# Eight gate units of the merge beside the last two RWKV pairs, and the pooling of the even layer beside its matrix units

## The reference

```python
# first block
proj = h @ w_in                         # attention, RWKV and gate columns
y_att  = attention_mixer(att_in) @ w_att_out
y_rwkv = rwkv7_mixer(rwkv_in, ...) @ w_rwkv_out
g_att, g_rwkv = split(sigmoid(gate_in + b_gate))
x = x + gt1 * ((g_att * y_att + g_rwkv * y_rwkv) @ w_o)
# ... conv ffn, norm; second block, layer 0 (the even layer)
proj = xn @ w_in_even                   # a_b, a_c, a_v (512 each), z_b (512)
y_a = a_b * causal_dwconv3(a_c * a_v, conv_w)
# y_b: for each of 4 groups of 128 channels, window w in (2, 4, 8, 16)
pooled = (cs - shifted) / minimum(pos, w) - z      # mean of the last w tokens, minus z
y_b = einsum(pooled, w_pool) * pool_scale
h = h + concat(y_a, y_b) @ w_out_even
```

## Time and profile before

| | us |
|---|---|
| median of 3 runs (lowest, highest) | 2472.72 (2471.85, 2472.84) |
| the profiled execution | 2470.49 |
| its span | 2469.3 |
| PE busy in the span | 2337.9 (95%) |
| DVE, POOL, ACT busy | 1433.1, 882.9, 686.1 |

### The profile page before, as it was taken

One profiled execution on the slowest core, in us unless ns is written; L12 is line 12 of the kernel. 1 busy time (PEld: TensorE's weight loads), 2 busy tenths in 40 slices (PEclk: granted clock), 3 DMA queues, 4 the chain that ended last, 5 costly groups with the idle time before them and its releaser, 6 DMA issues.

```text
span 2469.3 us, 33874 instructions
## 1 busy us (share of the span) xinstructions
PE 2337.9 (95%) x14384; PEld 1847.0 (75%) x14384; DVE 1433.1 (58%) x1805; ACT 686.1 (28%) x854; POOL 882.9 (36%) x415
## 2 busy tenths in 40 slices
PE   6999998999998799899999988999999999999998
PEld 4776775666665688678888866888888887888887
DVE  4221324577667411766675568888863457888733
ACT  3222113434442423222222221322222332322212
POOL 4322221111110344344444433444444444444443
PEclk8999999999999899989999989999999999999999
DMA  6433332212110333223333323233333322333331
GB/s 235 128 103 111 111 103 68 51 41 51 43 45 14 107 98 94 86 77 94 98 112 94 90 62 88 86 102 95 95 110 95 93 86 85 98 98 94 113 94 58
DMA packets 412038, 222.56 MB, mean 90 GB/s; under 512 B 33823, under 2 KB 409458, under 8 KB 410610
## 3 DMA queue, kind: packets, MB, share of 16 engines
q1 hardware_dynamic: 387234, 208.23, 29.2%
q10 hardware_dynamic: 24656, 12.18, 1.8%
HBM read 214.61 MB, written 5.77 MB: 89 GB/s over the span
## 4 chain that ended last, share of the span: by engine, by line
PE 59%; DVE 6%; issue 1%; ACT 1%; POOL 0%; DVEq 0%; ACTq 0%
PE bank L309 59%; DVE ev_s L2406 0%; DVE h_low L2014 0%; DVE mg_r_low L1992 0%; DVE g_c L2216 0%; PE bank L312 0%; DVE ev_low L2418 0%; DVE x_res L2363 0%; DVE sq L653 0%; DVE sq L649 0%; DVE ev_z L2373 0%; DVE ev_c L2375 0%; DVE ev_c L2382 0%; DVE ev_s L2409 0%; DVE sq L2113 0%
## 5 line engine op out<-in xcount | busy, mean ns | idle before, releaser
L305 POOL TENSOR_TENSOR w_low<-w_raw,w_high 128x1024 fp32r<-128x1024 f32 (+1 forms) x331 | 849.5, 2568 | 1494.7 <-ACT w_high L298 1494.6
L309 PE MATMUL bank<-h_high,w_high 128*128 128x512 f32 x2008 | 809.0, 403 | 28.4 <-DVE h_low L660 9.6
L309 PE MATMUL bank<-h_low,w_high 128*128 128x512 f32 x2008 | 789.3, 393 | 0.0
L298 ACT CAST w_high<-w_raw 128x1024 fp32r<-128x1024 f32 (+1 forms) x331 | 358.5, 1084 | 913.2 <-PE bank L309 899.6
L309 PE MATMUL bank<-h_high,w_low 128*128 128x512 f32 x2008 | 510.5, 394 | 0.0
L309 PEld LDWEIGHTS bank<-h_high,w_high 128*128 128x128 f32 x2008 | 379.9, 189 | 133.7 <-issue 24.8
L309 PEld LDWEIGHTS bank<-h_high,w_low 128*128 128x128 f32 x2008 | 377.0, 189 | 84.2 <-issue 4.6
L309 PEld LDWEIGHTS bank<-h_low,w_high 128*128 128x128 f32 x2008 | 381.3, 190 | 78.1 <-issue 3.4
L309 PE MATMUL bank<-g_high,w_high 128*128 128x512 f32 x352 | 138.1, 392 | 2.3 <-ACT g_c L2195 2.3
L309 PE MATMUL bank<-g_low,w_high 128*128 128x512 f32 x352 | 137.8, 391 | 0.0
L2092 DVE TENSOR_TENSOR x_res<-bank,x_res 128x512 f32<-128x512 f32 x32 | 22.1, 692 | 164.8 <-PE bank L309 164.8
(11 more groups left out here) (375 smaller groups left out, 2886.2 us busy)
## 6 DMA issues: line engine op xcount, KB each, us to landing
w_raw<-in_w_in SPq DMA_DIRECT2D x58, 512.0 KB, 4.7
w_raw<-in_w_up SPq DMA_DIRECT2D x44, 512.0 KB, 3.8
w_raw<-in_w_ffn_gate SPq DMA_DIRECT2D x44, 512.0 KB, 3.8
w_raw<-in_w_ffn_up SPq DMA_DIRECT2D x44, 512.0 KB, 3.8
w_raw<-in_w_ffn_down SPq DMA_DIRECT2D x32, 704.0 KB, 4.5
w_raw<-in_w_ada SPq DMA_DIRECT2D x32, 512.0 KB, 3.6
w_raw<-in_w_down SPq DMA_DIRECT2D x16, 704.0 KB, 4.5
w_raw<-in_w_in ACTq DMA_DIRECT2D x21, 512.0 KB, 4.1
```

Of the source, the lines that this page charges most:

```text
L298: self.A.copy(self.w_high[:, u % SPLIT_SLOTS, 0:k * P], self.raw_of(key)[:, 0:k * P]).then_inc(*self.S.rounded(*key))
L305: self.G.tensor_tensor(self.w_low[:, slot, 0:k * P], self.raw_of(key)[:, 0:k * P], self.w_high[:, slot, 0:k * P].bitcast(F32), ALU.subtrac ...
L309: return self.T.matmul(out, lhsT, rhs, start=start, stop=stop, skip_group_check=True)
```

## The change

**Merge.** The eight gates (n, 0) and (n, 1) for n = 0 to 3, called u = 0 to 7 here, come first in the order of units. u0 and u1 are woven in beside the chain and the mean of pair 6, u2 beside the solve of pair 7, u3 beside its chain, u4 beside its mean and variance (`EARLY`); u5 to u7 run right behind. Their sigmoids go to the tiles of `x` instead of `masks_room`. ACT's casts and sigmoids for them are placed by hand in `recurrence_act` and `merge_act`; POOL subtracts seven of them in the recurrence. The meetings of the engines before the merge go; each split is waited for by tile (`ready`), where it is used. The transfer of `x` waits for the fourth merged tile, `both` 3.

**Even layer.** The pooling of group g comes right behind its multiplication by the root; the table of counts becomes 16 reciprocals made at the start (`few`). The product with `w_pool` comes before the unit (n, 0); ACT makes the high parts of both results, DVE the low ones; the residual is scaled two tiles at a time; `even_out` takes tiles 4 to 7 first and no longer waits for ACT's last instruction. In `f_down`, `h_low` is written before the last scaling and squares.

Left out of the diff below: the declarations of tiles, the setup of `few` (POOL: one iota of 16 and four small copies at the start; DVE: one reciprocal of 128x64 with the RWKV vectors), and lines that only follow from those shown.

```diff
-        for n in range(DT):
...
-            unit(("merge", n, 3), wr, n * P)
+        for n, j in self.merge_order():
+            if j < 2:
...
         for n in range(4):
             for j in (1, 2, 0):
+                if j == 0:
+                    ring.append((("w_pool", n), [(0, 0, None, io["w_pool_2"][0, n])], None))
                 unit(("even", n, j), even, n * P + j * 4 * P)
-            ring.append((("w_pool", n), [(0, 0, None, io["w_pool_2"][0, n])], None))
...
+        order = self.TILE_ORDER.get(key[0], range(tiles))
...
     def recurrence_pe(self):
...
-        later = lambda i, j, b: self.projected_pe(i, j, b) if has(i) and i else iter(())
+        def later(i, j, b):
+            if has(i):
+                return self.projected_pe(i, j, b) if i else iter(())
+            return self.early_gate_pe(self.EARLY[i, j]) if (i, j) in self.EARLY else iter(())
...
+    GATES_EARLY = 8
+    EARLY = {(DT, IN_K): 0, (DT, IN_R): 1, (DT, IN_V): 2, (DT + 1, IN_K): 3, (DT + 1, IN_R): 4}
...
+    def merge_order(self):
+        early = [divmod(u, 2) for u in range(self.GATES_EARLY)]
+        return early + [(n, j) for n in range(DT) for j in range(4) if (n, j) not in early]
...
+    def early_gate(self, u):
+
+        return ("merge",) + divmod(u, 2), 7 - u % 2, self.x[:, u, :]
+
+    def early_gate_pe(self, u):
+        key, b, _ = self.early_gate(u)
+        self.empty(b)
+        yield from self.product_steps(key, self.bank[b][:], *self.h_parts())
+        self.emptied[b] = (self.S.gate_open, key[1:])
+        yield
...
+    def early_gate_act(self, u):
+        key, b, tile = self.early_gate(u)
+        _, n, j = key
+        if u == 0:
+            self.A.wait_ge(*self.S.dve_arrive.at("mixed", DT - 1))
+        self.A.wait_ge(*self.S.product.at(*key))
+        self.A.activation(tile, self.bank[b][:], ACT.Sigmoid, bias=self.col("b_gate", n + j * DT)).then_inc(*self.S.gate_open(n, j))
...
     def recurrence_act(self):
         has = self.has
         for i in range(-2, DT + 1):
             if has(i + 1):
                 self.rwkv_loads(("g2", i + 1), ("w2a2", i + 2), ("rwkv", i + 2, IN_K))
+            if i == DT - 2:
+                for u in range(3):
+                    self.load_gate(u)
             self.roots_act(i + 1, i - 1)
+            if i == DT - 1:
+                self.early_gate_act(1)
+                self.round_gate(3)
...
@@ -1863,7 +1919,17 @@
                 if has(i + 2):
                     self.round_unit(("rwkv", i + 2, IN_K))
                     self.rwkv_loads(("rwkv", i + 2, IN_V))
+                else:
+                    self.round_gate(0)
+                    self.load_gate(3)
                 self.arrive_act(i + 1)
+            if i == DT - 2:
+                self.round_gate(1)
+            if i == DT - 1:
+                self.early_gate_act(2)
+                self.round_gate(4)
+                self.early_gate_act(3)
+                self.round_gate(5)
             if has(i + 2):
                 if i >= -1:
                     self.round_unit(("rwkv", i + 2, IN_R))
@@ -1872,8 +1938,9 @@
                 self.values_act(i + 1)
             if has(i + 2) and i + 2:
                 self.round_unit(("rwkv", i + 2, IN_V))
-            if i == DT - 1:
-                self.round_unit(("merge", 0, 0))
+            if i == DT - 2:
+                self.early_gate_act(0)
+                self.round_gate(2)
         self.end("act", "rwkv")
...
-        self.lower_unit(("merge", 0, 0))
+        for u in range(7):
+            self.lower_unit(self.early_gate(u)[0])
...
-        self.meet("pe", "rwkv")
-        self.emptied = [None] * 8
-        for n in range(DT):
...
-                if n == 0 and j == 2:
-                    self.T.wait_ge(*S_.dve_merge.at("low", 10))
-                    self.T.wait_ge(*S_.pool_merge.at("low", 11))
...
+        for u in range(len(self.EARLY), self.GATES_EARLY):
+            run(self.early_gate_pe(u))
+        split = lambda i: [S_.pool_merge.at("low", i) if i % 3 == 2 else S_.dve_merge.at("low", i)]
+        ready = {(0, 2): split, (0, 3): lambda k: split(4 + k)}
+        for n, j in self.merge_order()[self.GATES_EARLY:]:
+            b = 4 * (n % 2) + j
+            self.empty(b)
+            self.product(("merge", n, j), self.bank[b][:], *parts[j], ready=ready.get((n, j)))
+            self.emptied[b] = (S_.dve_merge, ("both", n))
...
-        self.meet("act", "rwkv")
+        self.early_gate_act(4)
+        self.round_gate(6)
+        order = self.merge_order()
         for n, (high, low, src) in enumerate(self.merge_inputs()):
+            if n == 0:
+                A.wait_ge(*self.ended("pe", "rwkv"))
+            if n == 5:
+                self.early_gate_act(5)
+                self.round_gate(7)
+            if n == 11:
+                self.early_gate_act(6)
+                self.round_unit(("merge",) + order[8])
+                A.wait_ge(*self.ended("dve", "rwkv"))
...
+        self.early_gate_act(7)
+        for m in range(self.GATES_EARLY, len(order)):
+            n, j = order[m]
+            if m + 1 < len(order):
+                self.round_unit(("merge",) + order[m + 1])
+            else:
...
+                    A.wait_ge(*S_.dve_merge.at("both", n - 1))
...
-        self.meet("dve", "rwkv")
...
+            gates = [self.early_gate(2 * n + j)[2] if 2 * n < self.GATES_EARLY else self.gate[:, j, :] for j in range(2)]
+            for j, gate in enumerate(gates):
...
         for n, (high, low, src) in enumerate(self.merge_inputs()):
+            if n == 5:
+                self.lower_unit(self.early_gate(7)[0])
...
+        for key in self.merge_order()[self.GATES_EARLY:]:
+            self.lower_unit(("merge",) + key)
...
-        self.meet("pe", stage, ("act",))
+        if stage != "even":
+            self.meet("pe", stage, ("act",))
...
+            low = lambda: V.tensor_tensor(self.h_low[:, n, :], gained, self.h_high[:, n, :].bitcast(F32),
+                                          ALU.subtract).then_inc(*S_.h_low_even(to, n))
             if first:
                 self.add_square(self.rinv_first, x)
+                V.wait_ge(*S_.act_norm.at(to, "high", n))
+                low()
+                V.wait_ge(*self.own("dve"))
...
-            if to:
+            if to and not first:
                 V.wait_ge(*S_.act_norm.at(to, "high", n))
...
+                if j == 0:
+                    T.wait_ge(*S_.dve_even.at("pooled", n))
+                    T.wait_ge(*self.loaded(("w_pool", n)))
+                    self.empty(7)
+                    self.mm(self.bank[7][:], self.raw_of(("w_pool", n))[:, 0:P], self.e_zp[:, n, :], True,
+                            True).then_inc(*S_.plain_used("w_pool", n))
+                    self.emptied[7] = (S_.dve_even, ("parts", 4 + n))
...
+                    if n:
+                        self.even_high(n - 1)
+            A.wait_ge(*S_.plain_used.at("w_pool", n))
+            A.activation(self.e_high[:, 4 + n, :], self.bank[7][:], ACT.Copy, bias=0.0,
+                         scale=self.col("pool_scale_2", n)).then_inc(*S_.act_even("high", 4 + n))
+        self.even_high(3)
         self.end("act", "even")
+
+    def even_high(self, n):
+        self.A.wait_ge(*self.S.dve_even.at("out", n))
+        self.A.copy(self.e_high[:, n, :], self.e_z[:, n % 2, :]).then_inc(*self.S.act_even("high", n))
...
+            self.pool_dve(g)
...
-        V.wait_ge(*S_.pool_setup.at("positions"))
...
-            cnt = self.e_cnt[:, g, :]
...
-            V.reciprocal(cnt[:, 0:window], cnt[:, 0:window]).then_inc(*S_.dve_even())
-            V.memset(cnt[:, window:S], 1.0 / window).then_inc(*S_.dve_even())
-        for k in range(DT):
-            V.tensor_tensor(self.x[:, k, :], self.x[:, k, :], self.rinv_first[:], ALU.mult).then_inc(*S_.dve_even("residual", k))
...
-            self.pool_dve(n)
...
+            V.wait_ge(*S_.act_even.at("high", 4 + n))
+            V.scalar_tensor_tensor(self.e_low[:, 4 + n, :], self.bank[7][:], self.col("pool_scale_2", n),
+                                   self.e_high[:, 4 + n, :].bitcast(F32), ALU.mult,
+                                   ALU.subtract).then_inc(*S_.dve_even("parts", 4 + n))
...
+            if n < 3:
+                self.even_residual(n)
...
-            self.even_parts(n, z)
-            V.wait_ge(*S_.plain_used.at("w_pool", n))
-            V.wait_ge(*self.own("dve"))
-            V.tensor_scalar(self.e_s1[:], self.bank[7][:], self.col("pool_scale_2", n), None,
-                            ALU.mult).then_inc(*S_.dve_even("mixed", n))
-            self.even_parts(4 + n, self.e_s1[:])
+            V.wait_ge(*S_.act_even.at("high", n))
...
+        self.even_residual(3)
...
+        for k in (2 * n, 2 * n + 1):
+            self.V.tensor_tensor(self.x[:, k, :], self.x[:, k, :], self.rinv_first[:], ALU.mult).then_inc(*self.S.dve_even("residual", k))
...
-        V.tensor_tensor(src, src, self.e_cnt[:, g, :], ALU.mult).then_inc(*S_.dve_even())
```

(44 more changed lines are left out.)

71 lines of the change are left out of this document (18 added, 53 removed).

## The result

Over 4 runs each, the changed kernel takes **2434.77 us** (2432.54 to 2435.63) where the kernel before takes 2472.28 (2469.14 to 2472.84). The ratio is 0.9853, 95% interval 0.9841 to 0.9865: faster by 37.5 us. The forecast was 2424, the range 2416 to 2439. Sign and range hold. Of the 48.8 us of the sum, 35.8 arrived in the profiled spans (2469.3 to 2433.5). Thirteen are missing, and most of the experiments are about those.

A forecast was written before the change was run, and what follows sets the result against it. PE was seen busy almost everywhere, with idle time and low clock at the recurrence's end and in the even layer. Merge 27.2 plus even layer 4.5, 8.1 and 9.0 make 48.8; 2472.7 less that gives 2424, range 2416 to 2439.

The forecast's parts named there:

- Merge, step 1: Recurrence up to 802.6: solve of pair 7 starts unchanged; u0 and u1 fill the wait for inverses, costing nothing.
- Step 2: Solve of pair 7 with u2 woven in: 14.4 us instead of 10.2, so carry starts at 817.0, 4.2 later.
- steps 3 and 4: Pair 7's carry and chain with u3 end at 830.1; mean and variance with u4 take 7.4, to 837.5.
- step 5: u5 to u7 run dense for 16.3 us, to 853.8, covering the pair's close and all twelve splits.
- Step 6: Rest of the merge: four branch pairs 32.6 and four full output tiles 76.2 us, ending at 962.6.
- Even layer: Three gains in the even layer: h_low earlier 4.5, pools beside the pool units 8.1, the end 9.0 us.
- "nothing" for `few`: Setup of `few` at the start: a few small operations while PE waits for loads, counted as costing nothing.
- Gates delay more than they fill: Rival in the merge: hand-placed sigmoids and casts on ACT delay the path, 14 us lost, 2438; chance 0.14.
- DVE bound: Rival in the even layer: DVE needs 19 instead of 15.9 per n, 9 us lost, 2433; chance 0.12.
- Return of x: Rival in the merge: x's transfer not hidden, up to 8.9 us less the 1.0 counted, 2432; chance 0.06.
- Not effective: Rival: PE's order holds early gates back, merge brings 0, 21.6 us from the even layer remain, 2451; chance 0.04.
- Slower by the clock: Rival listed among the chances only as clock, its description and size not in the text given; chance 0.02.

The follow-up runs named there:

- the kernel with 64 bytes: Changed kernel plus an unused tile of 64 bytes per partition behind `few`, moving the later tiles; median 2436.5 us, ratio 0.9859 to the kernel before.
- the repetition: The changed kernel run once more, unaltered, on another occasion; median 2434.2 us, ratio 0.9856 to the kernel before.
- after with 192 bytes of room: Changed kernel plus an unused tile of 192 bytes per partition behind `few`; median 2424.1 us, ratio 0.9811 to the kernel before.
- a_room128: Changed kernel plus an unused tile of 128 bytes per partition behind `few`; median 2424.1 us, ratio 0.9807 to the kernel before.
- m_only: Only the recurrence and merge part of the change, on the kernel before, without `few`; median 2447.1 us, ratio 0.9903 to the kernel before.

## Why the prediction was right, and where it was off

**Right: what bounds the kernel, and what fills it.** The idle time of the last pair and of the even layer was the only thing to win, and early gates and pools beside units take it.

- *Merge, step 1* (solve of pair 7 stays at 802.6, loads on ACT's queue free) failed: 805.18. At 775 the changed kernel is 0.6 ahead, in spite of a wait of 1.30 for rw_sixteen at solve(6). From there it needs 3.2 more than before: 1.35 is the idle time at 780 beyond before's 0.25, and about 1.5 the clock of 0.50 for 3.4 us behind it (the kernel with 64 bytes has the same idle time of 1.60, keeps a clock of 1.00, and needs 1.5 less). The step looked at who waits for ACT and SP, not at PE's own instruction fetch, whose block starts at 3.16 instead of 1.68 with the 512 KB transfer beside it. Nor was there any slack to take it: PE is busy 18.34 of the 19.0 us from 786 to 805, and no wait for the inverses is left ahead of the solve. The two gates filled the cover whole, so each microsecond lost before it arrives at the solve.
- *Step 2* (14.4) measured 15.35; *steps 3 and 4* (20.5) 20.8 and *step 5* (16.3) 16.6, to the first branch product at 857.93, forecast 853.8. *Step 6* with x's return and hitches (110.3) measured 111.15, of which 0.7 is the place of mg_*.
- Together: wo's first product at 969.08 instead of 991.25 before: 22.2 of 27.2. The 5.0 that are missing are the 2.6 of step 1, the 0.95 of step 2, and 0.3, 0.3 and 0.85 in the steps behind it; in the run of the merge part alone the lead at wo was 25.9.
- *Half clock at wo*: not in the sum; 0.50 for 3.4 us and 1.4 lost in the profiled execution, 1.00 in the repetition.
- *Even layer:* the next unit starts at 1410.87, 4.9 earlier by the lead of 18.3 (forecast 4.5); the pools bring 31.4 - 18.3 - 4.9 = 8.2 (8.1); the end 41.0 - 31.4 = 9.6 (9.0). 22.7 of 21.6.
- *The term that was wrong:* "nothing" for `few`. Its instructions cost nothing that shows: the changed kernel is 0.6 ahead at 754. Its 320 bytes cost 8.4 by the steps, 10.6 by medians (after with 192 bytes of room), 8.9 on the kernel before.

The account of the profiled spans: 48.8, less 5.0 (merge), 1.4 (clock at wo), 7.9 (places behind the merge: 2.4 + 2.3 + 2.1 in the down projections, 0.6 + 0.5 in even_out and odd_out), plus 1.1 (even layer), leaves 35.6; measured 35.8.

**The range held in part by luck.** Its upper part was there for the first three rivals, and none of them came. The 2434.8 stands inside it for a reason that the prediction does not name, the place of the tiles. With that mended by 192 bytes the same change has a median of 2424.1, the forecast; but its profiled span gains 44.0 and not 48.8, so this agreement is closer than the sum deserves.

**The rivals.** *Gates delay more than they fill:* no. From solve to wo PE waits 1.05 for ACT, as it did before, 0.60 for a subtraction and 0.35 for a cast. *DVE bound:* no; it waits 7.8 us for PE over n = 1 to 3. *Return of x:* that 0.35, since the cast had waited for the 256 KB of (4, 2); 1.0 was forecast, and in most of the other traces it is nothing. *Not effective:* no. *Slower by the clock* (0.02 in the chances): no. From 745 to 1000 the granted clock was 0.50 twice, for 3.4 us each, from 781.0 and from 975.6, both times behind an idle time (1.60 and 2.41) and not among small steps, at a cost of some 2.9 us in all. The 336 matmuls of the eight gates and the four branch pairs ran at 1.00.

**The table load, and DVE beside POOL.** Timeline of ACT ahead of u6, after:

```profile
843.10 0.63 ACT L1319 ACTIVATE sq<-sq 128x512 f32<-128x512 f32 x1
843.75 1.28 ACT L1892 ACT_TABLE_LOAD   x1
845.05 0.69 ACT L1892 ACTIVATE x_res<-bank,vec 128x512 f32<-128x512 f32 x1
```

The load costs 1.28 between root and sigmoid, as in the kernel before, and PE did not wait for u6. Beside POOL's subtractions (2.38 to 2.86 each) DVE is held up as forecast: the four first additions of the pools took 2.42 each on average (L2495) and the four scalings of L2455 2.27 (0.75 once, 2.77 at most), where 0.69 and 0.75 is their time alone. The seven of these eight that took over 2 us, and one later addition (2.91), had started 0.03 to 0.67 behind the start of such a subtraction and ended 0.54 or 0.55 behind its end; so each cost 1.6 to 2.2, where 2.1 was forecast. For n = 1 to 3 DVE was busy 15.5, 13.2 and 12.1, against 15.9 forecast.

## What to carry to other kernels

A tile added to a long-lived allocation moves every tile behind it, here by its 320 bytes. Compare the step between matmul starts, tile by tile, before and after any change, also in stages that it does not touch; in this kernel the step was shortest (226.7 ns against up to 233.6) where moving tile and weights start at the same place modulo 256 bytes, so after such a change put them back there. When loads are moved to an idle queue, ask also which engine's instruction fetch falls beside them: here PE then idled 1.14 to 1.60 us instead of 0.25. And a gain under 3 us on this kernel is read from the trace at the place of the change: the four runs of `a_room128` lie 6.5 us apart at mean clocks of 0.986 to 0.983.

## What the runs showed of the hardware that was not expected

- For fp32 products of 128 x 128 weights and 128 x 512 moving data at a granted clock of 1.00, the step between matmuls is 226.7, 229, 232.4 to 233.6, or 233.3 to 233.5 ns where the moving tile starts 0, 64, 128 or 192 bytes (modulo 256) behind the weights' tile. All traces agree as far as the moving tile was shifted, but for even_out in m_only; that the weights' place counts as much rests on one trace. Why is open, and other distances were not tried.
- The wait for h_low inside wo (2.18 to 2.51 us) was followed, over the next 3.9 us, by a granted clock of 0.56 to 0.70 in seven traces (0.50 for 3.4 us; 1.4 or so lost) and of 1.00 in the other seven, in the changed kernel once each. The length of the wait does not tell them apart: 2.26 to 2.51 in the first, 2.18 to 2.51 in the second.
- At its idle time near 780 PE resumes 1.28 to 1.49 us behind the end of the 16 KB block of instructions that is fetched there, in thirteen traces. Beside a 512 KB weight load the block starts later (2.52 to 3.16 instead of 1.43 to 2.19 us behind the same product) but takes no longer. PE's idle time, which no semaphore explains, is 1.14 to 1.60 with the load and 0 to 0.78 without it.
